# Two first weight blocks multiplied chunk by chunk inside the modulation's entry, x laid out by partition, columns by 32-wide tiles

## What is computed

```python
c_act = jax.nn.silu(c)
for l in range(DEPTH):
    mod = c_act @ ada_w[l] + ada_b[l]
    (sh1, sc1, g1, sh2, sc2, g2, sh3, sc3, g3) = jnp.split(mod, 3 * N_SUBLAYERS, axis=-1)
    h = modulate(rms_norm(x, ffn1_norm[l]), sh1, sc1)     # h * (1 + scale) + shift
    x = x + 0.5 * g1[:, None, :] * swiglu(h, ffn1_w_gate[l], ffn1_w_up[l], ffn1_w_down[l])
    ...
```

## Time and profile before

| | |
|---|---|
| median of 3 runs | 1263.84 us |
| profiled execution, its own time | 1263.69 us |
| its span in the profile | 1261.7 us |
| TensorE (PE) busy | 1240.8 us, 98% of the span |
| VectorE (DVE) busy | 1001.3 us, 79% |
| ScalarE (ACT) busy | 602.3 us, 48% |
| mean granted clock of PE, as a share of full | 0.994 |
| `down(0)` of the first FFN starts at | 45.06 us |

### The profile page before, as it was taken

How to read it: one execution, slowest core, us unless ns; L and a number is a source line. 1 busy time by engine, 2 the same in 40 slices (tenths; PEclk the granted TensorE clock), 3 DMA queues, 4 the chain that set the end, 5 groups by cost and what they waited for, 6 DMA issues and landing times.

```text
span 1261.7 us, 26977 instructions
## 1 busy us (share of the span) xinstructions
PE 1240.8 (98%) x11512; PEld 1210.9 (96%) x11512; DVE 1001.3 (79%) x1633; ACT 602.3 (48%) x861; POOL 88.8 (7%) x159
## 2 busy tenths in 40 slices
PE   9999999999999999999999999999999999999997
PEld 7999999999999999999999999999999988999997
DVE  4899998787888667999988888899975858666665
ACT  4534334576333646443336675333353466543333
POOL 0111110000111040111110000000001000000000
PEclk9999999999999999999999999999998999999999
DMA  9999998442888653999994435545543522555550
GB/s 369 378 394 393 365 363 326 137 163 74 320 329 331 234 202 125 348 369 364 351 383 150 162 105 192 203 170 191 219 132 118 199 69 85 201 201 196 187 185 35
DMA packets 66103, 293.93 MB, mean 233 GB/s; under 512 B 7745, under 2 KB 8897, under 8 KB 51905
## 3 DMA queue, kind: packets, MB, share of 16 engines
q1 hardware_dynamic: 47552, 225.10, 49.3%
q0 software_dynamic: 18432, 67.12, 13.4%
HBM read 291.14 MB, written 1.05 MB: 232 GB/s over the span
## 4 chain that ended last, share of the span: by engine, by line
PE 89%; DVE 6%; ACT 3%; DMA 1%; issue 1%; SPq 0%; DVEq 0%; ACTq 0%
PE gu_bank L647 16%; PE gu_bank L648 16%; PE gu_bank L649 16%; PE y_bank L647 7%; PE y_bank L648 7%; PE y_bank L649 7%; PE t_bank L647 2%; PE t_bank L648 2%; PE t_bank L649 2%; DVE dn_lo L1815 1%; PE gu_bank L699 1%; PE gu_bank L703 1%; PE gu_bank L700 1%; DMA ring<-mix_w 1%; PE y_bank L673 1%
## 5 line engine op out<-in xcount | busy, mean ns | idle before, releaser
L647 PE MATMUL gu_bank<-hT_hi,gu_hi 128*128 128x256 f32 x1668 | 462.1, 277 | 3.5 <-DVE hT_lo L1801 1.6
L648 PE MATMUL gu_bank<-hT_lo,gu_hi 128*128 128x256 f32 x1668 | 461.4, 277 | 0.0
L649 PE MATMUL gu_bank<-hT_hi,gu_lo 128*128 128x256 f32 x1668 | 461.4, 277 | 0.0
L647 PEld LDWEIGHTS gu_bank<-hT_hi,gu_hi 128*128 128x128 f32 x1668 | 313.8, 188 | 4.5 <-issue 2.8
L649 PEld LDWEIGHTS gu_bank<-hT_hi,gu_lo 128*128 128x128 f32 x1668 | 313.9, 188 | 0.0
L648 PEld LDWEIGHTS gu_bank<-hT_lo,gu_hi 128*128 128x128 f32 x1668 | 313.9, 188 | 0.0
L1820 DVE TENSOR_TENSOR gu_lo<-raw_gu,gu_hi 128x2048 fp32r<-128x2048 f32 x103 | 236.3, 2294 | 38.0 <-ACT gu_hi L1334 35.9
L1334 ACT ACTIVATE gu_hi<-raw_gu 128x2048 fp32r<-128x2048 f32 x100 | 191.0, 1910 | 36.3 <-DMA raw_gu<-ffn_gu 36.3
L1351 ACT ACTIVATE sg<-gu_bank 128x256 f32<-128x256 f32 x88 | 33.8, 385 | 357.7 <-PE gu_bank L649 357.7
L647 PE MATMUL y_bank<-act_hi,dn_hi 128*128 128x256 f32 x660 | 183.0, 277 | 0.0
L648 PE MATMUL y_bank<-act_lo,dn_hi 128*128 128x256 f32 x660 | 182.3, 276 | 0.0
(11 more groups left out here) (504 smaller groups left out, 2130.0 us busy)
## 6 DMA issues: line engine op xcount, KB each, us to landing
raw_gu<-ffn_gu SPq DMA_DIRECT2D x110, 1024.0 KB, 6.7
stage<-ada POOLq DMA_DIRECT2D x128, 512.0 KB, 8.0
raw_dn<-ffn_dn SPq DMA_DIRECT2D x110, 512.0 KB, 3.7
ring<-mix_w SPq DMA_DIRECT2D x72, 512.0 KB, 3.7
stage<-ada SPq DMA_DIRECT2D x8, 512.0 KB, 14.3
pro<-ada SPq DMA_DIRECT2D x6, 512.0 KB, 13.0
x<-x_in SPq DMA_DIRECT2D x1, 1024.0 KB, 5.6
ring<-ada SPq DMA_DIRECT2D x2, 512.0 KB, 17.5
```

The costliest lines, as they stand in the source:

```text
L647: pe.matmul(to, a[0], b[0], start=start, stop=False)
L648: pe.matmul(to, a[0], b[1], start=False, stop=False)
L649: return pe.matmul(to, a[1], b[0], start=False, stop=stop)
```

## The change

Four things are changed, all of them in the first 70 us:

1. **Loads.** Block 0 of gate and up is asked for after the pieces of chunk 0, block 1 after those of chunk 2 (before: after chunk 1, and behind all pieces). Behind the last piece come down block 0, gate and up block 2, down block 1, and then the small tables. Down block 2 waits, as before, for the `lo` half of down block 0.
2. **Products.** PE multiplies both blocks chunk by chunk between `parts` and `part_columns`; `gate_up(1)` is gone. The 17 `idle_products` become 4. The splits of block 0 are made by halves, those of block 1 stand after chunk 2 on ACT and DVE, and the first down block is split on ACT before the last chunk. `rope_turns` moves from `beside(0)` to `beside(1)`.
3. **x** is stored in DRAM as partitions x chunks x tokens, so that a partition is one run of 8 KB instead of eight of 1 KB.
4. **Columns.** `part_columns` makes each column by four matmuls of 32 rows of output instead of one of 128.

```diff
             for c in range(KC):
                 columns_of(c)
                 columns_of(STAGES + c)
-                if c == 1:
-                    load_gu(0, 0)
-            load_gu(1, 1)
-            for g in range(2):
-                load_dn(g, g)
+                if c in (0, 2):
+                    load_gu(c // 2, c // 2)
+            load_dn(0, 0)
+            next_gu(0, 0, 0)
+            load_dn(1, 1)
...
             sp_.dma_start(pos_i, positions.to_broadcast([P, S])).then_inc(pos_loaded, 16)
+            next_dn(0, 0, 0)
...
                 for r in range(2):
-                    last = pe.matmul(yb[2 + c % 2][:, r:r + 1], mod_parts[:, c % 2, tok(r)], one_each, start=True, stop=True)
+                    for s in range(4):
+                        last = pe.matmul(yb[2 + c % 2][group(s), r:r + 1], mod_parts[:, c % 2, P * r + 32 * s:P * r + 32 * s + 32], one_each, start=True, stop=True)
...
             clear(gu_bank[0])
-            idle_products(17)
-            for c in range(2, KC - 1):
+            idle_products(4)
+            clear(gu_bank[1])
+            parts(2)
+            first_products(0, 0)
+            part_columns(2)
+            first_products(0, 1)
+            parts(3)
+            first_products(0, 2)
+            part_columns(3)
+            first_products(1, 0)
+            first_products(1, 1)
+            for c in range(4, KC - 1):
                 parts(c)
-                first_products(c - 2)
+                first_products(0, c - 1)
                 part_columns(c)
-            first_products(KC - 3)
+                first_products(1, c - 2)
             parts(KC - 1)
+            first_products(1, KC - 3)
             part_columns(KC - 1)
-            first_products(KC - 2)
-            first_products(KC - 1)
+            for c in (KC - 2, KC - 1):
+                first_products(0, c)
+                first_products(1, c)
...
             squares(0)
             parts_to_rows(0)
+            split_half(0, 0, 0)
             root(0)
+            split_half(0, 0, 1)
+            first_shifted(0)
             parts_to_rows(1)
-            split_block0(0)
-            first_shifted(0)
             first_shifted(1)
-            for c in range(2, KC):
+            parts_to_rows(2)
+            first_shifted(2)
+            table(ACT.Silu)
+            split_block1(0)
+            for c in range(3, KC):
                 parts_to_rows(c)
+                if c == KC - 1:
+                    first_dn()
                 first_shifted(c)
-            split_block1(0)
...
-                    if l == 0 and n == 0:
+                    if l == 0 and n == 1:
                         rope_turns()
...
             first_sums()
+            split_block0_half(0, 0)
             root(0)
             first_chunk(0)
-            split_block0(0)
-            first_chunk(1)
-            first_lo(0)
-            for c in range(2, KC):
-                first_lo(c - 1)
-                first_chunk(c)
-            first_lo(KC - 1)
-            for h in range(2):
-                split_block1(0, h)
+            split_block0_half(0, 1)
+            for c in range(KC):
+                if c:
+                    first_chunk(c)
+                first_lo(c)
+                if c == 2:
+                    for h in range(2):
+                        split_block1(0, h)
...
-        "x_in": a["x"][0].T, ...
+        "x_in": a["x"][0].T.reshape(KC, P, S).transpose(1, 0, 2), ...
```

More of the change, by code:

```diff
@@ L429, in load_dn, with next_gu, next_dn, next_block @@
                 sp_.dma_start(raw_dn[:, b, :], ffn_dn[g]).then_inc(dn_loaded[b], 16)
-            def next_block(base, n, b):
+            def next_gu(base, n, b):
                 sp_.wait_ge(gu_lo_done, base + n + 1)
                 load_gu(base + n + 2, b)
+            def next_dn(base, n, b):
                 sp_.wait_ge(dn_lo_done, base + n + 1)
                 load_dn(base + n + 2, b)
-            def ffn_loads(base):
-                for n in range(FB - 2):
+            def next_block(base, n, b):
+                next_gu(base, n, b)
+                next_dn(base, n, b)
+            def ffn_loads(base, first=0):
+                for n in range(first, FB - 2):
                     next_block(base, n, n % 2)
@@ L484, in _ @@
             sp_.dma_start(pos_i, positions.to_broadcast([P, S])).then_inc(pos_loaded, 16)
+            next_dn(0, 0, 0)
             for l in range(DEPTH):
-                ffn_loads(2 * FB * l)
+                ffn_loads(2 * FB * l, 1 - l)
                 units(mix_w, UNITS * l, range(RING), mixer_used(l))
@@ L723, in gate_up @@
                         pe.wait_ge(prod_done, base + n - 1)
-                    halves = f == 0 and n == 1
-                    pe.wait_ge(*((gu1_lo_half, 1) if halves else (gu_lo_done, base + n + 1)))
+                    pe.wait_ge(gu_lo_done, base + n + 1)
                     for h in range(2):
-                        if halves and h:
-                            pe.wait_ge(gu_lo_done, base + n + 1)
                         for c in range(KC):
@@ L762, in ffn @@
                     gate_up_first(kt, range(2 if pair else 1))
-                if not pair:
+                if f == NFFN - 1:
                     gate_up(1)
@@ L958, in sums_after_ffn, with first_products @@
                 pe.wait_ge(prod_done, FB * (f + 1))
-            def first_products(c):
-                pe.wait_ge(gu_lo_done, 1)
-                by_chunk(0, block_targets((0,)), (c,))
+            def first_products(b, c):
+                pe.wait_ge(gu_lo_done, b + 1)
+                by_chunk(0, block_targets((b,)), (c,))
             pe.wait_ge(ones_set, 3)
@@ L1351, in silu @@
                     act.activation(sg[:, b, :], gu_bank[b][:, 0:S], ACT.Silu).then_inc(silu_done, 1)
-                table(ACT.Silu)
-                if f == NFFN - 1:
+                if f:
+                    table(ACT.Silu)
+                if f in (0, NFFN - 1):
                     silu(0)
-                split_dn(0)
-                split_dn(1)
+                if f:
+                    split_dn(0)
+                    split_dn(1)
                 for n in range(FB - 2):
-                    if n or f < NFFN - 1:
+                    if n or 0 < f < NFFN - 1:
                         silu(n)
                     split_gu(n + 2)
-                    if n:
+                    if n or f == 0:
                         split_dn(n + 1)
@@ L1458, in first_shifted, with first_dn @@
                 act.activation(hT_hi[:, c, :], hT[:, c, :], ACT.Identity, bias=mods[:, KC + c:KC + c + 1]).then_inc(hT_hi_done, 1)
+            def first_dn():
+                act.wait_ge(dn_loaded[0], 16)
+                act.activation(dn_hi[:, 0, :], raw_dn[:, 0, :], ACT.Copy).then_inc(dn_hi_done, 1)
             def rope_tables(n):
@@ L1463, in rope_tables @@
                     act.activation(c_row[:, :], c_row[:, :], ACT.Silu).then_inc(c_ready, 1)
-                if n == 2:
+                if n == 3:
                     act.wait_ge(prep_args, 1)
@@ L1835, in split_block0_half @@
             def split_block0_half(f, h):
-                dve.wait_ge(*((gu0_hi_half, f // 2 + 1), (gu_hi_done, FB * f + 1))[h])
+                dve.wait_ge(*((gu0_hi_half, (f + 1) // 2 + 1), (gu_hi_done, FB * f + 1))[h])
                 lo_half(f, 0, h)
@@ L1887, in ffn @@
                 split_dn(0)
-                split_dn(1)
+                if f == 0:
+                    hidden(0)
+                if f:
+                    split_dn(1)
                 for n in range(FB - 2):
-                    if not (pair and n == 1) and (n or f < NFFN - 1):
+                    if not (pair and n == 1) and (n or 0 < f < NFFN - 1):
                         hidden(n)
@@ L2593 @@
     arrays = {
-        "x_in": a["x"][0].T, "positions": a["positions"], "consts": consts, "cols": cols, "rows": rows, "ada": ada,
+        "x_in": a["x"][0].T.reshape(KC, P, S).transpose(1, 0, 2), "positions": a["positions"], "consts": consts, "cols": cols, "rows": rows, "ada": ada,
         "ffn_gu": gu.reshape(NFFN * FB, P, 2 * KC * P), "ffn_dn": dn.reshape(NFFN * FB, P, D), "mix_w": mix, "mix2_w": mix2,
```

2 lines of the change are left out of this document (1 added, 1 removed).

## The result

The changed kernel takes 1268.8 us (median of 10 runs, 1264.98 to 1273.42); before took 1263.74 (10 runs, 1261.77 to 1264.42). The ratio is 1.0048, 95% interval 1.0036 to 1.0061: 0.5% slower (the medians alone give 1.0040). Before's runs lie 2.7 us apart, those of the changed kernel 8.5. The mean granted clock of the changed kernel's runs goes from 0.988 to 0.997, and its four slowest runs are at 0.988 to 0.991. The profiled execution is the slowest of the ten (1273.42, span 1271.4), so its rows show the dearest case.

A forecast was written before the change was run, and what follows sets the result against it. The prediction took PE to bound the first FFN behind 41 us, after an entry partly waiting for DMA. It summed 1263.69 + 3.0 (late `down(2)`) + 1.5 (clock fall) = 1268.2 us, range 1263.0 to 1271.0.

The forecast's parts named there:

- Loads and x: Entry's loads: pieces behind the two moved blocks land 2.5 us later less 0.4, the last at 33.0, at no cost.
- The 0.4 for x: Load of x at the start: longer runs save 0.4 us of 5.6, between 0 and 1.
- Start and loop: Entry: first product with block 1 at 27.5, turns of 3.06 us, `down(0)` at 45.3, 0.2 later than before.
- the rival of draining tiles: Entry loop: each tiling change costs 0.28 us instead of 0.1, entry 2.2 us longer, total 1270.4; chance 0.13.
- the clock in the entry: Entry: idle of 1.4 and 0.8 us at 25 to 27.5 noted; the one expected fall was put behind the stall.
- Block 3 and `rope_turns`: First FFN: late block 3 plus 4.69 us of `rope_turns` in block 1 make `down(2)` 3.0 us later, at 64.7.
- DVE is only 1.45 us early: Block 1 of the kernel before: DVE ends `hidden(2)` only 1.45 us before `down(2)` starts at 61.70.
- The fall behind the stall: Behind the idle stretch ahead of `down(2)`: one clock fall costing 1.5 us, bounds 0 and 3.0.
- the rival without a fall: Behind the stall ahead of `down(2)`: the clock does not fall, total 1266.7; chance 0.20.
- What bounds the kernel: First FFN: PE has no idle stretch of 0.3 us behind 41 us, so shifts there move the end equally.
- My rival of DMA's pace: Entry keeps up with the pieces, turns of 2.5 us; loads keep `down(2)` at 60.5, total 1262.5; chance 0.15.
- the 4.5 us of the forecast: Whole kernel: 3.0 us of stall ahead of `down(2)` plus 1.5 for the clock fall, over 1263.69.

The follow-up runs named there:

- e4: The changed kernel with 25 more idle matmuls in the gaps of its entry; 1267.55 us, ratio 1.0034.
- e8: e4 with whole 128-wide column products as before, without the 32-wide tiles; 1266.63 us, ratio 1.0023.
- e2: The changed kernel with `rope_turns` back in block 0 and ACT's tables moved along; 1266.14 us, ratio 1.0027.
- e3: The changed kernel with `rope_turns` in two parts beside blocks 2 and 4, ACT's tables moved along; 1269.2 us, ratio 1.0050.
- e5: e4 with gate-up block 3 asked for ahead of the wait for down block 0's split; 1265.4 us, ratio 1.0011.
- e6: e5 with `rope_turns` split over blocks 0 and 1; 1265.25 us, ratio 1.0013.
- e9: e5 with the three modulation columns beside block 1 put off to blocks 2 to 6; 1264.06 us, ratio 1.0010.
- e1: The kernel before with `rope_turns` alone moved to block 1 and ACT's sine tables one block later; 1263.95 us, ratio 1.0010.
- e7: The kernel before with 10 idle matmuls between the last chunks of its entry; 1262.02 us, ratio 0.9988.
- e12: The same kernel as e7, run once more for a second trace; 1262.16 us, ratio 0.9998.
- e11: The kernel before with only x laid out by partition, one 8 KB run each; 1262.53 us, ratio 0.9993.
- e10: e7 with gate-up block 2 asked for ahead of `c_row`, the constants and the positions; 1261.03 us, ratio 0.9986.

## Why the prediction was right, and where it was not

*The size and sign:* forecast 1268.2, measured 1268.8.

*Loads and x:* the last piece was forecast at 33.0 and landed at 32.93. The 0.4 for x is about right as an average (0.5), though the changed kernel's own trace shows nothing of it (5.6 us, as before). So that 33.0 was met to 0.1 us is in part luck.

*Start and loop:* the first product with block 1 at 27.5, a turn of 3.06, `down(0)` at 45.3. e4, at the full clock, has 27.59, 3.02 and 45.32. Columns were forecast at 0.22 and a change of mode at 0.1; they took 0.24 and 0.08. So the walk through the new order held, and the rival of draining tiles is out: e8 would have come to 2.6 us a turn and stayed at 3.06. The Trainium skill's page "TensorEngine Tiling (Array Packing)", section "Tiling Modes", has a change of mode drain the engine; the runs here put the price of entering the tiles at 0.08 us (0.88 against 0.80, e4 and e8).

*The failed step is the clock in the entry.* I counted the idle stretches (1.4 and 0.8 us at 25 to 27.5; 2.44 and 0.87 in the trace, and 2.05 and 1.00 ahead of them, which I had not) and gave the clock a fall only behind the stall. In the profiled execution two falls of 6.8 us put `down(0)` at 50.83, 5.5 us later than e4's 45.32. The traces show the term better than the times. With the gaps open the clock fell twice (changed kernel), twice (e2) and once (e3), and `down(0)` came at 50.83, 49.62 and 46.29. With idle matmuls in the gaps (e4, e5, e6, e8, e9) it stood at 1.00 from 12 to 46 us in all five traces, and `down(0)` came at 45.08 to 46.23. The average price is smaller than in the profiled execution: from e4 to the changed kernel the ratio goes from 1.0034 to 1.0048, 1.8 us, and the intervals overlap. The spread of the runs is no clean sign of it: 8.5 us (ten runs of the changed kernel) and 5.8 (six of e3) with the gaps open, but 3.7 (six of e2), as in e4 (3.8, five).

What I passed over is the first gap, which comes from the new order of the loads. Block 0 is now asked for ahead of the pieces of chunk 1, so PE starts on that chunk's `parts` at 14.67 and not at 12.79, behind 2.05 us of waiting for `pro<-ada`, and the first fall begins at 16.0. The 13 idle matmuls that the change took away aren't what opened that gap: they stood behind the columns of chunk 1, which is at 18.5 us in the changed trace, later than the first fall's start, and no gap is there.

*Block 3 and `rope_turns`:* DVE was to start on block 3 at 51.8 and PE to idle 2.7 us ahead of `down(2)` at 64.7; e4 has 51.65, 2.34 and 64.38. e1 shows that the new place of `rope_turns` alone costs nothing behind `down(0)`, e5 that the late issue is 1.4 of the 2.3 us, e2 that the old place doesn't free the changed kernel. "DVE is only 1.45 us early" was the number that mattered.

*The fall behind the stall:* forecast 1.5; 1.93 and 1.90 were lost from `down(2)` to `down(3)` in e4 and the changed kernel. e8 has one too, behind 2.42 us. Behind e5's 0.91 us of idle time there was none, nor behind e2's 1.21. For a stall as long as the changed kernel's the rival without a fall is out in all three traces.

*What bounds the kernel:* "whatever shifts PE there shifts the end by as much" holds for a delay and not for a gain. e7, e12 and e11 reached `down(0)` 0.4 to 1.5 us early and had lost it by `down(5)`, where all stand at 86.1 to 86.7. For block 2's load this is tried: e10 moved it alone and kept 1.2 us. That the later losses (0.6 us from `down(3)` to `down(4)` in e12, where VectorE had waited 2.36 us for block 5's weights) come from the loads too is read from the trace and not tried. My rival of DMA's pace used this floor for the changed kernel alone; it is in before too.

*Sum:* the 4.5 us of the forecast stand against 4.3 by e4's ratio, with the entry's clock held, and 5.1 (medians) to 6.1 (ratio) for the changed kernel. What was missing is the entry's clock; for the rest, 2.7 us up to `down(2)` instead of 3.0 and 1.9 for the fall instead of 1.5 (e4) nearly cancel, which is luck in the sum. Why one execution draws two falls in the entry and another a single shorter one stays open: the same instructions met both (changed kernel, e2, e3), and only filling the gaps was tried.

## What to carry to other kernels

Spreading a phase's matmuls over its wait gains only if what the tail hid (here the first hidden block, a table load, the split of down block 0) stays hidden, and if no load queues behind an event that the change makes later: read SP's queue for every wait that moved. Work moved from a block with slack to the next one is free only while that block's weights are on time, and it must be measured together with the loads. A gap on PE can cost more than its length (in e4 1.93 us of lower clock behind 2.34 of idle time), and filling the entry's gaps with idle matmuls cost nothing that the traces show and held its clock in all five of them; but a gain at one place has to be followed to the next floor before it is counted.

## What the runs showed of the hardware that I had not expected

A single idle gap of 2.34 us (e4), 2.42 us (e8) or 1.99 us (changed kernel), with PE busy ahead of it, was followed at once by 3.4 us at the lower level; one of 0.91 us (e5) or 1.21 us (e2) was not. But length alone doesn't decide: e3's entry has gaps of 1.96 and 1.23 us at 14 to 17 us and stays at 1.00 up to 26.9, where the changed kernel's (2.05 and 1.00) were met by a fall at 16.0. 1 MB in runs of 8 KB landed after 5.2 us on average, in runs of 1 KB after 5.7. And a load of 1 MB of gate-up weights took from 5.6 us from issue to landing (block 3 in the changed kernel, issued after a stretch with a DMA share of 0.01) over 13.3 (block 3 in e9) to 18.1 (block 2 in e10), the last two issued into a stretch with a share of 1.02.
